# First attention: GpSimd in place of VectorE multiplies the probabilities by the inverse of their sum

## Chip, core and metric

One core of a Trainium2 chip (trn2) runs the whole program in one launch. The metric is the device time of one execution in microseconds (us). The kernel before takes 2439.32 us, the median of 3 runs (2437.27 to 2439.40).

## What is computed

A first network of two layers (grouped attention with a sink and a context, then a retention layer, each with a gated feed-forward part and adaptive modulations), followed by a second network of two layers. The change concerns the attention of the first layer of the first network, for 256 tokens, 16 heads of 64 and 4 key heads. The softmax has one more term, the sink, in its sum. The image tokens look at 512 keys, the context tokens at 256.

```python
s_ctx = jnp.einsum('bqkgd,bnkd->bkgqn', qb, k_c, preferred_element_type=jnp.float32) * scale
s_loc = jnp.einsum('bqkgd,bnkd->bkgqn', qb, kb, preferred_element_type=jnp.float32) * scale
s_loc = jnp.where(valid, s_loc, NEG_INF)
sink_col = jnp.broadcast_to(sink_g, s_ctx.shape[:-1] + (1,))
p = jax.nn.softmax(jnp.concatenate([s_ctx, s_loc, sink_col], axis=-1), axis=-1).astype(vb.dtype)
return (jnp.einsum('bkgqn,bnkd->bqkgd', p[..., :L], v_c)
        + jnp.einsum('bkgqn,bnkd->bqkgd', p[..., L:L + band], vb))
...
s_c = jnp.einsum('bqkgd,bnkd->bkgqn', q_c, k_c, preferred_element_type=jnp.float32) * scale
p_c = jax.nn.softmax(jnp.concatenate([s_c, sink_col], axis=-1), axis=-1).astype(v_c.dtype)
o_c = jnp.einsum('bkgqn,bnkd->bqkgd', p_c[..., :L], v_c)
```

## The kernel before

The program is written by hand, one instruction stream for each engine, and the streams meet at semaphores. SyncE streams the weights into four slots; ScalarE and VectorE split each into a high and a low part (lines 1653 and 2275); TensorE multiplies (lines 1060 to 1071). The attention stands between the query projection `q0` and the output projection `wo0`.

`heads_first` (line 617) lists the work of the first attention as blocks: for each of 8 pairs of heads one block for the image tokens (512 keys) and one for the context tokens (256 keys). A block has two steps, one for each half of 128 queries, and a step has two items, one for each head of the pair. So there are 32 steps and 64 items; of four steps in a row two are 512 keys wide and two 256. All four engines run the same function `attention`, each its own part, over the steps s; an engine works on several steps at once, by the lags `N_LAG` = 1, `T_LAG` = 2, `O_LAG` = 4 (line 677):

- **TensorE** (line 1252): scores of step s into three banks of PSUM used in turn; in every odd step side products of the modulation weights (line 1154, until these run out); the transposes of the probabilities of step s - 2 (line 1270, `wk` for the first item and `acc` for the second), which wait for `pn_ok` of their item; in every even step the product with the values (line 1288).
- **VectorE**: copies the sinks beside the probabilities' tile (line 2431), scales and masks the scores and takes their maximum in one instruction for each item (line 2440, into `probs`), makes the negative maximum (line 2444, two inputs in SBUF); then, for step s - 1, the reciprocal of the sums (line 2453, `rec_ok`) and, for each item, the multiply of the probabilities by it, in place (line 2459, `pn_ok`). The order of the instructions on the engine is that of the code.
- **ScalarE**: copies the transposed probabilities of step s - 2 out of PSUM (line 1859, `pt_ok`), then takes the exponentials of step s and their sum (line 1841, `p_ok`).
- **GpSimd** has nothing in this stretch. Behind it in its queue stand the sums of squares of `wo0` (`both_squares`, line 925), which wait for ScalarE's squares of that projection, and DMAs that follow these.

`probs` has 6 tiles, three steps of items. VectorE may write step s into them when the transposes of step s - 3 are done (`t_ok`, line 2431 waits). The inverse sums `srec` are a ring of 8. In the second network the same function runs again, with `again` true; there GpSimd makes the bias tiles (line 978) beside it, and VectorE's multiply stays as it is.

Of the kernel before, what the change touches and what calls it, by code (L numbers as in the profile page):

```python
# [23 lines left out]
ALU = mybir.AluOpType  # L24
# [328 lines left out]
PROBS, PROBS_T, SINK = 6, 4, 4  # L353
# [22 lines left out]
def pooled_both(name, n):  # L376

    return 5 * BOTH.index(name) + 2 * n + 1


def squared_before(name, l):

    first = [5 if n in BOTH else 4 for n in SQUARED1]
    if name in SQUARED1:
        return sum(first[:SQUARED1.index(name)])
    return sum(first) + 4 * SQUARED2.index(name) + l * 4 * len(SQUARED2)


def build(nc, a, out, const_at):
    J = JOBS  # L390
    st = ExitStack()
    with st:
        def sb(name, shape, dt=F32, on=st):
            return on.enter_context(nc.sbuf_tensor(name, shape, dt))

        def sem(name):
            return st.enter_context(nc.semaphore(name))
# [42 lines left out]
        smx, snm, ssum, srec = [sb(f"soft_{k}", [P, 8]) for k in ("mx", "nm", "sum", "rec")]  # L440
# [6 lines left out]
        def arena(*parts):  # L447
            with ExitStack() as on:
                return [sb(n, s, d, on) for n, s, d in parts]
# [4 lines left out]
        nf, nf_c, rows_c, prm_rows, ada_in, _, ada_s, c_pad, extra = arena(  # L454
            ("nf", [P, DC, S], F32), ("nf_c", [P, DC, S], F32), ("rows_c", [P, 2 * D], F32), ("prm_rows", [P, 4, P], F32),
            ("ada_in", [P, 2 * SLOTS, KCH, COLS], F32), ("ada_skip", [P, 592], F32), ("ada_s", [P, 4, COLS], F32),
            ("c_pad", [P, DC, 62], F32), ("extra", [P, EXTRA, KCH, COLS], F32))
# [5 lines left out]
        probs_t, probs = arena(("p_skip", [P, 10 * 2 * S + 4 * 256 + 4 * 2 * S], F32), ("probs_t", [P, PROBS_T, 4, S], F32),  # L463
                               ("probs", [P, PROBS, 2 * S + SINK], F32))[1:]
# [76 lines left out]
        s_ok, m_raw, m_ok, p_ok, rec_ok, pn_ok, t_ok, pt_ok, neg_ok = [sem(k) for k in (  # L541
            "s_ok", "m_raw", "m_ok", "p_ok", "rec_ok", "pn_ok", "t_ok", "pt_ok", "neg_ok")]
# [74 lines left out]
        def heads_first():  # L617

            bs = []
            for p in range(HEADS // 2):  # L620
                for ctx in range(2):
                    keys = slice(S, 2 * S) if ctx else slice(0, 2 * S)
                    tiles = range(2, 4) if ctx else range(4)
                    o = o_ps[p % 2]
                    gs = []
                    for n in range(2):
                        h, half = 2 * p + n, slice(64 * n, 64 * n + 64)
                        gs.append(dict(
                            q=[qk[half, p, ctx * S + r * P:ctx * S + (r + 1) * P] for r in range(2)],
                            k=[k_dup[half, h // GROUP, keys]] * 2, nk=[keys.stop - keys.start] * 2, rows=[slice(0, S)] * len(tiles), mask=[window[:, r, keys] for r in range(2)],  # L630
                            sink=(sinks, sinks_neg, 2 * p), scale=[q_inv[:, 2 * ctx + r, h:h + 1] for r in range(2)], probs=probs, probs_t=probs_t, pair=p,
                            v=[v_tok[:, t, 64 * (h // GROUP):64 * (h // GROUP) + 64] for t in tiles],
                            out=o[half, ctx * S:(ctx + 1) * S]))
                    bs.append((gs, [(p, o[:, 0:2 * S], h_hi[:, p, :], h_lo[:, p, :])] if ctx else []))
            return bs
# [34 lines left out]
        def attn_base(which, l):  # L670

            if which == "first":
                return 0, 0, 0
            return ITEMS0 + l * (ITEMS_WIN + ITEMS_MEM), PAIRS0 + l * (PAIRS_WIN + PAIRS_MEM), BLOCKS0 + l * BLOCKS2
# [4 lines left out]
        def attn_steps(blocks):  # L679
            return range(2 * len(blocks) + L_LAG - 1)  # L680
# [196 lines left out]
        def _(pool):  # L877
# [34 lines left out]
            pool.dma_start(window[:].rearrange("p r k -> p (r k)"), const("window")).then_inc(in_attn, 16)  # L912

            pool.wait_ge(x_done, X_START)
            def both_squares(name):

                k = pooled_both(name, 0)
                for n in range(3):
                    pool.wait_ge(sqb_ok, squared_before(name, None) + n + 1)
                    for c in range(2):  # L920
                        if n == 0 and c == 0:
                            continue
                        if n:
                            pool.wait_ge(both_ok, k + 2 * n - 2 + c)
                        pool.tensor_tensor(sq_total, act_buf[:, c, :], sq_total if n else act_buf[:, 0, :], ALU.add).then_inc(both_ok, 1)
# [34 lines left out]
            for l in range(LAYERS2):  # L960
# [4 lines left out]
                first, _, _ = attn_base("second", l)  # L965
# [1304 lines left out]
        def _(dve):  # L2270
# [146 lines left out]
            def attention(which, blocks, l=None, beside=None, ready=None):  # L2417
                first, pair0, _ = attn_base(which, l)
                again = which != "first"
                steps = 2 * len(blocks)  # L2420
                for s in attn_steps(blocks):
                    if s < steps:
                        gs, _ = blocks[s // 2]
                        i, c, sink = 2 * s, 2 * s % 8, gs[0]["sink"]
                        if i >= PROBS or again:
                            dve.wait_ge(t_ok, first + i - PROBS + 2)
                        if not s:
                            dve.wait_ge(*ready)
                        if sink is not None:
                            nk = gs[0]["nk"][s % 2]  # L2430
                            dve.tensor_copy(gs[0]["probs"][:, i % PROBS:i % PROBS + 2, nk:nk + 1], sink[0][:, sink[2]:sink[2] + 2].unsqueeze(2))
                        for n, G in enumerate(gs):
                            k = c + n
                            dve.wait_ge(s_ok, first + i + n + 1)
                            if again and G["bias"] is not None:
                                dve.wait_ge(bias_ok, 1 + G["bias"] + l * WH)
                            if again:
                                dve.memset(passed[:, k:k + 1], 0.0)

                            dve.tensor_tensor_reduce(G["probs"][:, (i + n) % PROBS, 0:G["nk"][s % 2]], (sc_ps[n] if again else sc_first[(i + n) % 3])[:, 0:G["nk"][s % 2]], G["mask"][s % 2], G["scale"][s % 2],  # L2440
                                                     -3.0e38, ALU.add, ALU.max, smx[:, k:k + 1]).then_inc(m_raw, 1)
                        dve.wait_ge(m_raw, first + i + 2)
                        if sink is not None:
                            dve.scalar_tensor_tensor(snm[:, c:c + 2], smx[:, c:c + 2], -1.0, sink[1][:, sink[2]:sink[2] + 2], ALU.mult, ALU.min)\  # L2444
                                .then_inc(m_ok, 2)
                        else:
                            dve.tensor_scalar(snm[:, c:c + 2], smx[:, c:c + 2], -1.0, None, ALU.mult).then_inc(m_ok, 2)
                    t = s - N_LAG
                    if 0 <= t < steps:
                        gs, _ = blocks[t // 2]  # L2450
                        j, k = 2 * t, 2 * t % 8
                        dve.wait_ge(p_ok, first + j + 2)
                        dve.reciprocal(srec[:, k:k + 2], ssum[:, k:k + 2]).then_inc(rec_ok, 2)
                        for n, G in enumerate(gs):
                            j = 2 * t + n
                            k = j % 8
                            dve.wait_ge(rec_ok, first + j + 1)
                            pr = G["probs"][:, j % PROBS, 0:G["nk"][t % 2]]
                            dve.tensor_scalar(pr, pr, srec[:, k:k + 1], None, ALU.mult).then_inc(pn_ok, 1)
                    q = block_at(s, L_LAG, blocks)  # L2460
                    if q is not None:
                        for pair, o, hi, lo in blocks[q][1]:
                            dve.wait_ge(o_hi_ok, pair0 + pair + 1)
                            dve.tensor_tensor(lo, o, hi, ALU.subtract).then_inc(o_done, 1)
                    if beside:
                        beside(2 * s)
                        beside(2 * s + 1)
# [228 lines left out]
            for j in range(STAGES):  # L2696
                dve.wait_ge(ada_sum, j + 1)
                stage_modulations(j)
                for kc in range(2 * j, 2 * j + 2):
# [5 lines left out]
                    for half in range(2):  # L2705
                        dve.wait_ge(nh_ok, 2 * kc + half + 1)
                        t = slice(half * S, half * S + S)
# [52 lines left out]
            n = [1]  # L2760
# [391 lines left out]
```

## Time and profile before

| | |
|---|---|
| median of 3 runs | 2439.32 us (2437.27 to 2439.40) |
| the profiled execution, its span | 2440.7 us, 1.4 above the median |
| TensorE busy | 2382.8 us (98%) |
| VectorE busy | 1560.6 us (64%) |
| ScalarE busy | 1213.9 us (50%) |
| GpSimd busy | 158.3 us (6%) |
| first attention | from 118 to 225 us of the span |

The profile is one execution with every instruction's start and duration. Busy is the time in which an engine has an instruction under way. The matmuls of TensorE overlap one another and their ends are modelled, so for TensorE the start of the next instruction tells more than a duration. "Idle before, released by" names the instruction whose semaphore came last. The chain is followed back from the last instruction of a stretch. Lines are those of the kernel before; in the changed kernel the lines of VectorE stand 13 further down. PE is TensorE, PEld its weight loads, DVE VectorE, ACT ScalarE, POOL GpSimd and SP SyncE.

### The profile page before, as it was taken

How to read it: one execution, taken by the hardware profiler on the slowest of the kernel's cores; microseconds unless marked ns; L12 is line 12 of the kernel's file. 1: busy time of each engine (PE TensorE's matmuls, PEld its weight loads, DVE VectorE, ACT ScalarE, POOL GpSimd, SP SyncE). 2: the span in 40 equal slices, each digit the busy share in tenths (PEclk: the TensorE clock that was granted, in tenths of full speed). 3: DMA queues.
4: the chain of work that ended last, by engine and by line, in shares of the span. 5: the costliest groups of instructions: out<-in, count | busy, mean ns of one | idle time of the engine just before them, and what ended most of it. 6: DMA issues, size and time to landing. Idle time of an engine off the chain costs nothing.

```text
span 2440.7 us, 39475 instructions
## 1 busy us (share of the span) xinstructions
PE 2382.8 (98%) x14178; PEld 2039.3 (84%) x14178; DVE 1560.6 (64%) x2316; ACT 1213.9 (50%) x1784; POOL 158.3 (6%) x145
## 2 busy tenths in 40 slices
PE   7999999999999999999999999999999999999999
PEld 6745788888788868888888899998888889989887
DVE  5377556432453366766876858777677766677774
ACT  4366422222343434555554586555455556865553
POOL 3000100000000000000000012100000000221000
PEclk9999999999999999999999999999999999999999
DMA  9453755433242424655656655456566565535654
GB/s 315 139 187 109 231 154 163 147 106 95 88 129 93 140 70 148 199 165 187 203 170 194 190 166 172 130 173 190 178 190 189 177 196 166 180 127 153 200 169 150
DMA packets 388418, 398.36 MB, mean 163 GB/s; under 512 B 17344, under 2 KB 382432, under 8 KB 388304
## 3 DMA queue, kind: packets, MB, share of 16 engines
q1 hardware_dynamic: 381984, 377.67, 50.4%
q0 software_dynamic: 6320, 19.17, 2.6%
q8 instruction: 72, 1.18, 0.2%
q14 instruction: 42, 0.34, 0.0%
HBM read 395.73 MB, written 1.05 MB: 163 GB/s over the span
## 4 chain that ended last, share of the span: by engine, by line
PE 87%; DVE 5%; issue 3%; ACT 2%; POOL 2%; DMA 0%; SPq 0%; ACTq 0%; DVEq 0%; POOLq 0%
PE acc L1060 29%; PE acc L1071 24%; PE acc L1064 18%; PE wk L1135 2%; PE acc L1135 2%; DVE w_lo L2275 1%; PE wk L1252 1%; ACT w_hi L1653 1%; PE acc L1605 1%; PE acc L1288 1%; PE wk L1288 1%; PE wk L1270 1%; PE wk L1154 1%; POOL bias L978 1%; PE wk L1496 1%
## 5 line engine op out<-in xcount | busy, mean ns | idle before, releaser
L2275 DVE TENSOR_TENSOR w_lo<-raw,w_hi 128x1024 fp32r<-128x1024 f32 (+1 forms) x656 | 816.0, 1258 | 503.8 <-ACT w_hi L1653 502.3
L1653 ACT CAST w_hi<-raw 128x1024 fp32r<-128x1024 f32 (+1 forms) x650 | 663.2, 1033 | 477.0 <-PE acc L1071 362.8
L1060 PE MATMUL acc<-h_all,w_hi 128*128 128x512 f32 x2328 | 586.0, 393 | 3.1 <-DVE h_all L2403 2.3
L1071 PE MATMUL acc<-h_all,w_lo 128*128 128x256 f32 (+1 forms) x3688 | 572.7, 298 | 0.0
L1071 PEld LDWEIGHTS acc<-h_all,w_lo 128*128 128x128 f32 x3688 | 525.2, 191 | 43.4
L1060 PEld LDWEIGHTS acc<-h_all,w_hi 128*128 128x128 f32 x2328 | 419.1, 189 | 80.4 <-issue 2.5
L1064 PE MATMUL acc<-h_all,w_hi 128*128 128x256 f32 (+1 forms) x2720 | 472.0, 326 | 10.6 <-DVE rot L2614 4.8
L1064 PEld LDWEIGHTS acc<-h_all,w_hi 128*128 128x128 f32 x2720 | 407.1, 192 | 55.6 <-issue 14.6
L1060 PE MATMUL acc<-hid_all,w_hi 128*128 128x512 f32 x880 | 221.5, 392 | 0.0
L1060 PEld LDWEIGHTS acc<-hid_all,w_hi 128*128 128x128 f32 x880 | 156.8, 188 | 26.8
L1071 PEld LDWEIGHTS acc<-hid_all,w_lo 128*128 128x128 f32 x1056 | 152.6, 188 | 17.0
L1071 PE MATMUL acc<-hid_all,w_lo 128*128 128x256 f32 (+1 forms) x1056 | 166.2, 297 | 0.0
L2572 DVE TENSOR_TENSOR act_buf<-acc,act_buf 128x512 f32<-128x512 f32 x110 | 76.0, 691 | 83.4 <-ACT act_buf L1935 54.0
L1064 PE MATMUL acc<-hid_all,w_hi 128*128 128x512 f32 x352 | 84.6, 392 | 0.0
L1935 ACT COPY act_buf<-acc 128x512 f32<-128x512 f32 x55 | 32.3, 587 | 95.3 <-PE acc L1071 95.3
L1064 PEld LDWEIGHTS acc<-hid_all,w_hi 128*128 128x128 f32 x352 | 66.0, 188 | 14.3
L1841 ACT ACTIVATE probs<-probs,soft_nm 128x257 f32<-128x257 f32 (+3 forms) x112 | 61.5, 554 | 21.2 <-DVE soft_nm L2444 18.1
L946 POOL TENSOR_TENSOR act_buf<-act_buf 128x512 f32<-128x512 f32 x8 | 10.4, 1299 | 860.6 <-ACT act_buf L1899 860.6
L2575 DVE TENSOR_TENSOR act_buf<-act_buf,rstd 128x512 f32<-128x512 f32 x88 | 60.9, 692 | 3.0
L1933 ACT COPY act_buf<-acc 128x512 f32<-128x512 f32 x55 | 32.2, 585 | 59.6 <-PE acc L1071 59.6
L1135 PE MATMUL wk<-w_hi,h_all 128*128 128x512 f32 x192 | 60.7, 393 | 0.1
L1945 ACT CAST hid_all<-act_buf 128x512 f32 (+1 forms) x55 | 34.2, 622 | 47.1 <-DVE act_buf L2580 46.3
(429 smaller groups left out, 2281.3 us busy)
## 6 DMA issues: line engine op xcount, KB each, us to landing
raw<-in_w_in_dram SPq DMA_DIRECT2D x100, 512.0 KB, 4.0
raw<-in_ffn_w_in_dram SPq DMA_DIRECT2D x88, 512.0 KB, 4.2
raw<-in_ffn_w_gate_dram SPq DMA_DIRECT2D x88, 512.0 KB, 4.4
raw<-in_ffn_w_up_dram SPq DMA_DIRECT2D x88, 512.0 KB, 4.3
raw<-in_ffn_w_down_dram SPq DMA_DIRECT2D x80, 512.0 KB, 4.1
raw<-in_ret_w_qkvg_dram SPq DMA_DIRECT2D x48, 512.0 KB, 3.7
raw<-in_ffn_w_out_dram SPq DMA_DIRECT2D x40, 512.0 KB, 3.5
ring<-in_ada_w_dram SPq DMA_DIRECT2D x34, 512.0 KB, 4.8
```

Source lines behind the costliest of these rows:

```text
L1060: pe.matmul(outs[cb], w_hi[:, s, k, c], merged[:, :, kk, t], start=(u == 0 and k == 0), stop=False, skip_group_check=True)
L1064: pe.matmul(outs[cb], w_hi[:, s, k, c], x[:, kk, t], start=(u == 0 and k == 0 and x is hi), stop=False, skip_group_check=True)
L1071: mm = pe.matmul(o, w_lo[:, s, k, cb * P:(cb + 1) * P], x[:, u * KCH + k, t], start=False, stop=(last and k == nk - 1), skip_group_check=True)
L1135: mm = pe.matmul(banks[n], xs[:, kk, x], ws[:, 2 * u:2 * u + 2, k, :], start=(kk == 0 and i == 0), stop=(kk == DC - 1 and i == 2))
L1288: mm = pe.matmul(G["out"][:, seen], G["v"][c], G["probs_t"][:, 2 * (q % 2) + n, c, seen], start=(c == 0), stop=(c == tiles - 1), skip_grou ...
L1653: act.copy(w_hi[:, s, 0:nk, :], raw[:, s, 0:nk, :]).then_inc(hi_done, 1)
L1841: act.activation(pr, pr, ACT.Exp, bias=snm[:, i % 8:i % 8 + 1], accum_out=ssum[:, i % 8:i % 8 + 1])\
L1935: act.copy(up, acc[:, 1, :, S:2 * S]).then_inc(low_ok, 1)
L1945: act.copy(hid_hi[:, bass.ts(it, 2), 0:S], buf).then_inc(hid_hi_ok, 1)
L2275: dve.tensor_tensor(w_lo[:, s, 0:nk, :], raw[:, s, 0:nk, :], w_hi[:, s, 0:nk, :], ALU.subtract).then_inc(lo_done, 1)
L2572: dve.tensor_tensor(part, acc[:, b, :, 0:S], part, ALU.add).then_inc(acc_free, 1)
L2575: dve.tensor_tensor(part, part, scale, ALU.mult).then_inc(gu_ok if b else gz_ok, 1)
```

## The change

GpSimd gets, after its last DMAs of the preparation, a loop over all 64 items of the first attention. For each it waits until the reciprocal is there (`rec_ok`), multiplies the item's probabilities in place, and reports it (`pn_ok`). VectorE skips its multiplies when the attention is the first, and with them its own wait for the reciprocal. TensorE waits for the same semaphore as before, at the same values.

```diff
             pool.wait_ge(x_done, X_START)
+
+            def normalise_first(blocks):
+
+                for t in range(2 * len(blocks)):
+                    gs, _ = blocks[t // 2]
+                    for n, G in enumerate(gs):
+                        j = 2 * t + n
+                        pool.wait_ge(rec_ok, j + 1)
+                        pr = G["probs"][:, j % PROBS, 0:G["nk"][t % 2]]
+                        pool.tensor_scalar(pr, pr, srec[:, j % 8:j % 8 + 1], None, ALU.mult).then_inc(pn_ok, 1)
+
+            normalise_first(heads_first())
+
             def both_squares(name):
...
                         dve.wait_ge(p_ok, first + j + 2)
                         dve.reciprocal(srec[:, k:k + 2], ssum[:, k:k + 2]).then_inc(rec_ok, 2)
-                        for n, G in enumerate(gs):
+                        for n, G in enumerate(gs if again else []):
                             j = 2 * t + n
                             k = j % 8
                             dve.wait_ge(rec_ok, first + j + 1)
```

On VectorE, before, where a step of 512 keys is followed by steps of 256 (`soft_nm` is the negative maximum, `soft_rec` the inverse sum; ISA is the instruction of line 2440, its second row the read of the maximum):

```order
L2444 SCALAR_TENSOR_TENSOR soft_nm<-soft_mx,sinks_neg 128x2
L2453 RECIPROCAL soft_rec<-soft_sum 128x2
L2459 TENSOR_SCALAR probs<-probs,soft_rec 128x512 x2
L2431 COPY probs<-sinks 128x2
L2440 ISA probs,soft_mx<-acc,act_buf,q_inv 128x256
L2440 ISA soft_mx 128x1
L2440 ISA probs,soft_mx<-wk,act_buf,q_inv 128x256
```

And the same place now:

```order
L2457 SCALAR_TENSOR_TENSOR soft_nm<-soft_mx,sinks_neg 128x2
L2466 RECIPROCAL soft_rec<-soft_sum 128x2
L2444 COPY probs<-sinks 128x2
L2453 ISA probs,soft_mx<-acc,act_buf,q_inv 128x256
L2453 ISA soft_mx 128x1
```

The two multiplies between the reciprocal and the next step's copy are gone; the rest keeps its order. On GpSimd, before, at the end of its preparation:

```order
L911 DMA sin_a<-in_shape_constants_dram 128x256
L912 DMA act_buf<-in_shape_constants_dram 128x1024
L925 ISA
L925 TENSOR_TENSOR rows<-act_buf 128x512 [waits sqb_ok,x_done]
L925 TENSOR_TENSOR rows<-act_buf,rows 128x512 [waits both_ok,sqb_ok]
```

And now (the squares follow after all 64 multiplies):

```order
L924 ISA
L924 TENSOR_SCALAR probs<-probs,soft_rec 128x512 [waits rec_ok,x_done]
L924 TENSOR_SCALAR probs<-probs,soft_rec 128x512 [waits rec_ok] x3
L924 TENSOR_SCALAR probs<-probs,soft_rec 128x256 [waits rec_ok] x4
L924 TENSOR_SCALAR probs<-probs,soft_rec 128x512 [waits rec_ok] x4
```

The multiplies stand in the queue ahead of the squares, each with a wait of its own.

## Rows read from the trace of the kernel before

**Rows 1.** The page, span and busy time of each engine with its share

```profile
span 2440.7 us, 39475 instructions
...
PE 2382.8 (98%) x14178; PEld 2039.3 (84%) x14178; DVE 1560.6 (64%) x2316; ACT 1213.9 (50%) x1784; POOL 158.3 (6%) x145
```

**Rows 2.** Chain of waits through the first attention, 118 to 225 us

```profile
by line: PE wk L1252 13.7%; PE wk L1270 12.3%; PE acc L1288 10.9%; PE wk L1288 10.8%; DVE probs L2440 10.8%; PE acc L1154 9.0%; PE acc L1252 8.3%; PE acc L1270 7.8%; DVE probs L2459 4.1%; issue 3.4%; PE wk L1154 1.9%; DVE soft_rec L2453 1.3
```

**Rows 3.** Windows: length, busy us of PE, PEld, DVE, ACT, POOL, clock, DMA

```profile
150.00:161.76 11.76, 11.56 (x100) 6.13 (x98) 9.63 (x38) 8.61 (x26) 0.00 (x0) 1.00 0.75 244
```

**Rows 4.** Timeline of TensorE, one pair: start us, us, instruction

```profile
147.99 0.44 PE L1270 MATMUL wk<-ident,probs 128*128 128x128 f32 x2
...
150.45 1.13 PE L1252 MATMUL wk<-k_dup,qk 64*128 64x512 f32 x4
...
152.51 0.44 PE L1270 MATMUL wk<-ident,probs 128*128 128x128 f32 x2
...
153.99 0.66 PE L1270 MATMUL wk<-ident,probs 128*128 128x128 f32 x4 [0.20 <-DVE probs L2459]
154.49 0.60 PE L1270 MATMUL acc<-ident,probs 128*128 128x128 f32 x4
...
157.66 0.66 PE L1270 MATMUL wk<-ident,probs 128*128 128x128 f32 x4
158.16 0.60 PE L1270 MATMUL acc<-ident,probs 128*128 128x128 f32 x4
```

**Rows 5.** Timeline of VectorE, the same stretch

```profile
146.31 0.62 DVE L2459 TENSOR_SCALAR probs<-probs,soft_rec 128x256 f32<-128x256 f32 x2
...
149.93 0.62 DVE L2459 TENSOR_SCALAR probs<-probs,soft_rec 128x256 f32<-128x256 f32 x2
...
151.61 0.75 DVE L2440 CUSTOM_DVE_ANT_0 probs<-wk,act_buf,q_inv 128x512 f32<-128x512 f32 x1 [0.39 <-PE wk L1252]
...
153.25 0.17 DVE L2453 RECIPROCAL soft_rec<-soft_sum 128x2 f32<-128x2 f32 x1
153.45 0.88 DVE L2459 TENSOR_SCALAR probs<-probs,soft_rec 128x512 f32<-128x512 f32 x2
...
155.62 0.88 DVE L2459 TENSOR_SCALAR probs<-probs,soft_rec 128x512 f32<-128x512 f32 x2
```

**Rows 6.** Waits in the first attention: total us, times, longest us

```profile
PE wk L1270 <- DVE probs L2459: 3.4, 8, 0.9
...
PE wk L1252 <- DVE soft_mx L2440: 1.6, 1, 1.6
```

**Rows 7.** Groups by line and shape: count, busy us, mean ns, idle before

```profile
L2459 DVE TENSOR_SCALAR probs<-probs,soft_rec 128x512 f32<-128x512 f32 x32 | 14.1, 484 | 0.7 <-DVE soft_rec L2453 0.2
...
L946 POOL TENSOR_TENSOR act_buf<-act_buf 128x512 f32<-128x512 f32 x8 | 10.4, 1299 | 860.6 <-ACT act_buf L1899 860.6
...
L964 POOL TENSOR_TENSOR GI<-GI,XC 128x2048 f32<-128x2048 f32 x2 | 9.2, 4623 | 230.4 <-ACT gates L1990 230.4
```

**Rows 8.** Timelines of GpSimd and VectorE in the second network's attention

```profile
1513.90 2.04 POOL L978 TENSOR_TENSOR bias<-alibi,slopes 128x512 f32<-128x512 f32 x2 [5.59 <-DVE soft_mx L2440]
...
1511.42 0.16 DVE L2444 SCALAR_TENSOR_TENSOR soft_nm<-soft_mx,sink_neg_l 128x2 f32<-128x2 f32 x1
...
1513.73 0.08 DVE L2440 DVE_READ_ACCUMULATOR2_ANT soft_mx<- 128x1 f32 x1
1513.93 1.02 DVE L2444 SCALAR_TENSOR_TENSOR soft_nm<-soft_mx,sink_neg_l 128x2 f32<-128x2 f32 x1
...
1515.06 1.15 DVE L2459 TENSOR_SCALAR probs<-probs,soft_rec 128x128 f32<-128x128 f32 x2
...
1526.50 0.48 DVE L2459 TENSOR_SCALAR probs<-probs,soft_rec 128x128 f32<-128x128 f32 x2
```

**Rows 9.** Timelines of GpSimd and TensorE at the last branch product

```profile
1581.98 1.56 POOL L983 TENSOR_TENSOR h_all<-gates,h_all 128x512 fp32r<-128x512 f32 x1 [1.30 <-ACT h_all L2019]
...
1583.67 1.57 PE L1064 MATMUL acc<-h_all,w_hi 128*128 128x256 f32 x11 [1.00 <-POOL h_all L983]
```

## Prediction

> **What bounds the kernel now.** I read the page first, then the stretch of the first attention (118 to 225 us), then one period of it instruction by instruction. The span is 2440.7 us, and GpSimd works 158.3 us of it, 6% [rows 1]. The change touches nothing outside the first attention, so its effect is a few us or parts of one per step, summed over the 32 steps.
>
> The chain through that stretch is mostly TensorE: score, transpose and value matmuls (lines 1252, 1270, 1288) and the side products (1154). VectorE is on it with the maxima (2440, 10.8%) and with the multiply that is moved (2459, 4.1%) [rows 2]. One pair of heads is four steps and repeats every 11.76 us; in the window of one such period TensorE is busy 11.56, VectorE 9.63, ScalarE 8.61 and GpSimd 0.00 us [rows 3]. So TensorE is the bound, and VectorE is not, although it is busy 82%.
>
> The reader should see how TensorE meets the multiply. In each step it writes scores, runs side work, and only then transposes the probabilities of two steps back. Take the pair whose second scores start at 150.45. The group of transposes at 153.99 is the one place of the four where TensorE is late on VectorE: its row says 0.20 idle, released by line 2459 [rows 4]. On VectorE the maxima start at 151.61 (after 0.39 of idle, so VectorE itself waited for scores), the reciprocal at 153.25 and the two multiplies at 153.45, 0.88 together [rows 5]. The first ends at 153.45 + 0.48 = 153.93, TensorE starts 0.06 later. In all, TensorE waits for line 2459 only 3.4 us here, and 1.6 us once for a maximum near the start [rows 6].
>
> **What is removed.** VectorE loses 64 multiplies: 16 steps of 0.88 and 16 of 0.62, that is 24.0 us of its busy time [rows 5, 7]. I cost that at nothing. Maxima cannot start before their scores, VectorE already idles before them, and the scores are in TensorE's order behind transposes and side work. If this cover is wrong, the most to gain is the waits on VectorE just named, 3.4 + 1.6 = 5.0 us, 0.2%. The additions below eat them first.
>
> **What is added.** GpSimd gets the same 64 multiplies, each waiting for the reciprocal. Nothing else stands in its queue meanwhile: the next thing there is the squares of the output projection, after attention. No DMA is moved past it, the SP queue is unchanged. The price is the latency from reciprocal to transpose. It is the sum of three things:
> - VectorE to GpSimd: a maximum read out at 1513.73 for 0.08 released GpSimd at 1513.90, so 0.09 us [rows 8].
> - D, the duration of one 128x512 multiply on GpSimd. No row shows a tensor_scalar there.
> - GpSimd to TensorE: the add at 1581.98 takes 1.56 and the matmul starts at 1583.67, so 0.13 us, where VectorE had 0.06 [rows 9].
>
> **D bounded.** From above by the two-input product or sum of the same shape, 1.30 [rows 7]. From below by VectorE's own 0.48; nothing excludes that GpSimd is as quick. Between them are two better guides. The bias (line 978) is also a tile times one value per partition, issued with that value as a second, repeated input: two take 2.04, so 1.02 each [rows 8]. And two-input ops of 512 and 2048 columns take 1.30 and 4.62 [rows 7]: 2.16 ns a column over 0.19 fixed. If one input costs half of that per column, D is 0.19 + 512 x 1.08 = 0.74, an estimate. I take the middle of 0.74 and 1.02, D = 0.88.
>
> The Trainium skill, "GPSIMD Engine Reference", section 4.1, puts one-input work on GpSimd roughly at line rate, and section 3.1 gives 1.03 cycles an element at 1.2 GHz for short bodies. By that figure D would be an estimated 0.44 plus the fixed part, 0.63, and the sum would be about 3 us instead of 7. No row here shows it, since every GpSimd row has two inputs.
>
> **The sum.** In the pair above the reciprocal ends at 153.25 + 0.17 = 153.42. GpSimd starts at 153.51 (0.06 after VectorE did), ends the second multiply at 153.51 + 2D, and TensorE can transpose that item at 153.64 + 2D. Before, it did so at 154.49 [rows 4]. The delay per pair is 2D - 0.85. (The first item gives D - 0.35, which is smaller once D is over 0.50.) With D = 0.88 this is 0.91 us per pair.
>
> The other three groups have slack. The second 128x512 group (multiplies at 155.62, transposes at 157.66 and, for its second item, 158.16) would be ready at about 155.68 + 1.76 + 0.13 = 157.57. The first 128x256 group (146.31, transposes 147.99, second item 0.27 later) with 0.54 each is ready at 146.37 + 1.08 + 0.13 = 147.58. The last (149.93, transposes 152.51) has over a microsecond more [rows 4, 5]. So one group in four pays.
>
> Seven pairs pay: 7 x 0.91 = 6.4 us. The first pair is different: TensorE waits there for a later maximum, behind six small rope products of VectorE that now need not wait for two multiplies (0.88 less) but partly stand behind GpSimd (below); I put it at 0, from -0.5 to +0.7. The last pairs have no side products to cover a group: there one more may pay the difference of the multiplies, 0.88 - 0.48 = 0.40, so +0.4, an estimate. The sum is +6.8 us. TensorE is the bound from there to the end, so all of it arrives. Against the span it gives 2447.5; the runs' median is 1.4 below the span, so 2439.3 + 6.8, rounded to **2446.0 us**.
>
> **GpSimd and VectorE hold each other up.** When the bias started at 1513.90, VectorE's 128x2 line 2444, which takes 0.16 otherwise, took 1.02, and the two 128x128 multiplies behind it 1.15 in place of 0.48 [rows 8]. With the change such a stall can fall on line 2444 of the next step: its two maxima take at least 0.96 us, GpSimd is busy 1.76 after the reciprocal, so VectorE stands some 0.3 to 0.8 us. This delays only exponentials and multiplies with 0.6 us of slack or more, and VectorE has just given up 0.62 to 0.88 in each step. I cost it at 0 with D = 0.88.
>
> **Rivals.**
> 1. *GpSimd is quick, D from 0.48 to 0.68.* For: one input instead of two. Against: no row below 1.02. The sum is 7 x (2D - 0.85) + 0.4, so +1.2 to +4.0 us: 2440.5 to 2443.3, no change. Chance 0.32. This is where the page's rate lands.
> 2. *Slow, and the lock bites.* D = 1.30, as with two inputs. Per pair 1.75; then the slack of the second 128x512 group is gone too (155.68 + 2.60 + 0.13 = 158.41 against 158.16) and the stalls of line 2444 join: 7 x 1.75 + 1 to 3 = 13 to 15 us, 2453 to 2454. For: the lock is in the trace. Against: the bias takes 1.02. Chance 0.10. The Trainium skill, "SBUF — State Buffer", section "Who interferes with whom", states that the second to issue blocks fully; by that the trace agrees (1.02 for 0.16), and it adds copies to the ops that can be held, which no run here shows.
> 3. *Faster.* The mechanism is VectorE's relief at the start and in the steps without side products: line 2459 no longer stands before the maxima that TensorE waits for (1.6 us once), and per pair 0.2 us of wait is won. It decides if D is under 0.43, where 2D - 0.85 turns negative and the two multiplies beat VectorE's 0.88. Then up to 5.0 us come back: about 2435. Against: VectorE's own instruction takes 0.48. Chance 0.05.
> 4. *The change does not move the work:* the order of instructions shows 32 pairs gone from VectorE and 64 on GpSimd, so no chance is kept for this.
>
> **How the numbers follow.** Forecast case, D from 0.68 to 1.15, +4 to +11 us, mostly slower by over 0.2% (4.9 us, about what a measurement of this kernel can tell from no change): chance 0.53. Its low end, D under 0.74, stays within 4.9 us and gives 0.05 to "same". Slower: 0.48 + 0.10 = 0.58. Same: 0.32 + 0.05 = 0.37. Faster: 0.05. The range runs from the lower bound of D, 2440.5, to 2452.5, just short of the two-input price; it leaves out rivals 2 and 3 and little else.
>
> **What would show it.** In the changed profile: 64 multiplies on GpSimd, none of line 2459's on VectorE in the stretch; their start-to-start time in a step is D. The wait of line 1270's transposes for GpSimd should be near 0.2 + 0.9 once a pair at the first 128x512 group, the period 12.7 instead of 11.76 us, VectorE's busy time 24 us lower, and line 2444 should have single instances near D. The prediction is wrong if the period stays 11.8 (D small), if transposes wait in more than one group of four, or if a later stretch takes the delay back.

## The result, and the profile after

The changed kernel takes **2463.32 us** (median of 4 runs, 2462.65 to 2466.57) against 2439.36 for the kernel before on the same chip (4 runs). The ratio is 1.0098, with a 95% interval of 1.0085 to 1.0111: slower by 24 us. The forecast was 2446.0 with a range up to 2452.5, so the direction came true and the size did not; the loss is 3.6 times what was forecast (24.0 against 6.7).

The head of the changed kernel's page, which answers to [rows 1]:

```profile
span 2461.3 us, 39475 instructions
...
PE 2389.8 (97%) x14178; PEld 2042.2 (83%) x14178; DVE 1539.1 (63%) x2252; ACT 1215.3 (49%) x1784; POOL 237.0 (10%) x209
```

The span is 20.6 us longer. The 64 instructions have moved (DVE x2316 to x2252, POOL x145 to x209). VectorE gave up 21.5 us, and GpSimd took on 78.7.

The groups by line and shape of the changed kernel in its first attention (118 to 250 us); columns: count, busy us, mean ns of one, idle before and its releaser:

```profile
L924 POOL TENSOR_SCALAR probs<-probs,soft_rec 128x512 f32<-128x512 f32 x32 | 49.6, 1566 | 88.5 <-DVE soft_rec L2466 88.5
L924 POOL TENSOR_SCALAR probs<-probs,soft_rec 128x256 f32<-128x256 f32 x32 | 29.2, 926 | 21.6 <-DVE soft_rec L2466 21.6
```

This is the term that the forecast did not have a row for: D is **1.57 us**, not 0.88, and above even the two-input instruction that was taken as the upper bound, 1.30 [rows 7]. In 256 columns it takes 0.93 where VectorE took 0.31 (two in 0.62, [rows 5]).

TensorE's waits in that stretch (total us, times, longest), to be held against [rows 6]; the transposes are now line 1283, the maxima 2453, the reciprocal 2466:

```profile
PE wk L1283 <- POOL probs L924: 13.3, 9, 2.0
PE acc L1283 <- POOL probs L924: 7.9, 11, 0.9
```

Together 21.2 us of waiting for GpSimd, where TensorE had waited 3.4 + 1.6 = 5.0 us for VectorE. The windows of two periods, columns as in [rows 3]:

```profile
167.10:181.15 14.05, 11.83 (x98) 6.10 (x97) 7.01 (x31) 8.88 (x27) 9.89 (x9) 1.00 0.31 103
181.15:195.20 14.05, 11.84 (x98) 6.11 (x97) 6.96 (x30) 8.83 (x27) 9.84 (x9) 1.00 0.00 1
```

A pair takes 14.05 us instead of 11.76, at the same granted clock, 1.00. TensorE is busy 11.84 of it, and no engine is busy throughout: the period is now set by a chain, not by an engine. One such period in detail, TensorE first (start, us, instruction, idle before and its releaser), to be held against [rows 4]:

```profile
185.83 0.66 PE L1283 MATMUL wk<-ident,probs 128*128 128x128 f32 x4 [1.33 <-POOL probs L924]
187.37 0.66 PE L1283 MATMUL acc<-ident,probs 128*128 128x128 f32 x4 [0.88 <-POOL probs L924]
...
190.61 0.66 PE L1283 MATMUL wk<-ident,probs 128*128 128x128 f32 x4
```

and VectorE and GpSimd in the same period:

```profile
183.95 0.17 DVE L2466 RECIPROCAL soft_rec<-soft_sum 128x2 f32<-128x2 f32 x1
...
185.53 0.16 DVE L2457 SCALAR_TENSOR_TENSOR soft_nm<-soft_mx,sinks_neg 128x2 f32<-128x2 f32 x1
```

```profile
184.21 6.19 POOL L924 TENSOR_SCALAR probs<-probs,soft_rec 128x512 f32<-128x512 f32 x4 [1.74 <-DVE soft_rec L2466]
```

The reader should see the chain: reciprocal ends at 184.12, GpSimd starts at 184.21 (0.09, as forecast), its first multiply is done after 6.19/4 = 1.55 at 185.76, and TensorE starts at 185.83. The second multiply ends at 187.31 and TensorE's second group starts at 187.37. The next row of 512 keys (190.61) does not wait: GpSimd has finished it at 190.40. So the forecast's picture, one exposed group in four, is what the trace shows: of the 20 waits on GpSimd above, 16 are the two items of the eight exposed groups. The other four, 1.7 us together, are the second item of a 256 group at 149.27 (0.20), of a 512 group at 218.56 (0.19), and a 256 group near the end (0.83 and 0.47, shown further down).

### The profile page after: what moved, and what is told of

Read it like the earlier page. It is cut to its first block, busy times and chain, and to the rows that moved or that the text cites. A ratio compares the mean times of both kernels' runs of the same rounds, so it can differ in the third digit from the quotient of the medians.

```text
span 2461.3 us, 39475 instructions
## 1 busy us (share of the span) xinstructions
PE 2389.8 (97%) x14178; PEld 2042.2 (83%) x14178; DVE 1539.1 (63%) x2252; ACT 1215.3 (49%) x1784; POOL 237.0 (10%) x209
## 3 DMA queue, kind: packets, MB, share of 16 engines
HBM read 395.73 MB, written 1.05 MB: 161 GB/s over the span
## 4 chain that ended last, share of the span: by engine, by line
PE 85%; DVE 5%; issue 3%; POOL 3%; ACT 2%; SPq 1%; DMA 1%; ACTq 0%; DVEq 0%; POOLq 0%
PE acc L1073 30%; PE acc L1084 24%; PE acc L1077 17%; PE wk L1148 2%; PE acc L1148 2%; POOL probs L924 1%; SPq L780 1%; DVE w_lo L2288 1%; PE wk L1265 1%; PE acc L1618 1%; ACT w_hi L1666 1%; PE wk L1301 1%; PE acc L1301 1%; DVE probs L2453 1%; POOL bias L991 1%
## 5 line engine op out<-in xcount | busy, mean ns | idle before, releaser
L924 POOL TENSOR_SCALAR probs<-probs,soft_rec 128x512 f32<-128x512 f32 (+1 forms) x64 | 78.8, 1246 | 110.1 <-DVE soft_rec L2466 110.1
```

What stands on the lines that cost most here:

```text
L924: pool.tensor_scalar(pr, pr, srec[:, j % 8:j % 8 + 1], None, ALU.mult).then_inc(pn_ok, 1)
```

## The experiments

The theory: the loss is the latency from the reciprocal to the first group of 512 keys in each pair, 2D - 0.85 a pair with D = 1.55 (the pitch of two multiplies). The rivals: the sum of 64 slow multiplies wherever they stand, including a second group of 512 whose slack is gone; contention between GpSimd and VectorE that makes D what it is; and the change of VectorE's order.

**1. Another form of the same multiply.** All 64 stay on GpSimd, as a product of two tensors, the second being the column repeated:

```diff
-                        pool.tensor_scalar(pr, pr, srec[:, j % 8:j % 8 + 1], None, ALU.mult).then_inc(pn_ok, 1)
+                        pool.tensor_tensor(pr, pr, srec[:, j % 8:j % 8 + 1].broadcast_to((P, G["nk"][t % 2])), ALU.mult).then_inc(pn_ok, 1)
```

> All 64 multiplies stay on GpSimd, but as a tensor_tensor whose second input is the inverse sum repeated along the row, the form of the bias op that took 1.02 us. Duration theory (the loss is the time of one GpSimd multiply in the latency from reciprocal to transpose, 2D - 0.85 a pair): D 1.02 to 1.3 instead of 1.57, so period 12.9 to 13.5 us instead of 14.05 and +10 to +15 us over before, not +24. Lock theory (the loss is VectorE and GpSimd holding each other up at the shared port, per instruction): as many instructions hold it, with two streams instead of one, so +20 us or more. Clock theory (waits of TensorE bring its clock down and that makes a good part of the loss): waits still come in every pair, so low stretches remain and the time stays over +15.

Measured: 2452.01 us against 2439.94, ratio 1.0047 [1.0031, 1.0064]. Half of the loss is gone (12.1 us left). Its groups and waits in the same stretch:

```profile
L924 POOL TENSOR_TENSOR probs<-probs,soft_rec 128x512 f32<-128x512 f32 x32 | 32.7, 1046 | 96.4 <-DVE soft_rec L2466 96.4
L924 POOL TENSOR_TENSOR probs<-probs,soft_rec 128x256 f32<-128x256 f32 x32 | 18.9, 612 | 31.2 <-DVE soft_rec L2466 31.2
```

```profile
PE wk L1283 <- POOL probs L924: 9.1, 9, 1.5
PE acc L1283 <- POOL probs L924: 2.9, 8, 0.5
```

With two inputs the same product takes 1.05 us, as the bias did [rows 8]. The period is 12.92 (from 163.67 to 176.59), 1.16 more than before; 2 x 1.02 - 0.85 gives 1.19, with 1.02 the pitch of two. The formula holds at a second value of D. The 12.1 us lie in the range of the duration theory, and below what the lock theory (+20 or more) and the clock theory (over +15) of the expectation asked for. This run also shows what the forecast expected of the lock. VectorE's timeline while two multiplies of GpSimd are under way (166.72 to 168.76):

```profile
166.72 2.04 POOL L924 TENSOR_TENSOR probs<-probs,soft_rec 128x512 f32<-128x512 f32 x2 [2.34 <-DVE soft_rec L2466]
```

```profile
168.05 0.72 DVE L2457 SCALAR_TENSOR_TENSOR soft_nm<-soft_mx,sinks_neg 128x2 f32<-128x2 f32 x1
```

That instruction, 0.16 otherwise, ends when the second multiply does. In the changed kernel itself its like at 185.53 took 0.16 in the middle of GpSimd's work (above).

**2 and 3. Only one of the two lengths on GpSimd.** VectorE keeps the others, in its old place; a second semaphore tells the two apart. The function's return value chooses the steps, and only this line differs between runs 2, 3, 5 and 6:

```diff
+        def pooled_item(t, n):
+            return t // 2 % 2 == 0
...
+                        if not pooled_item(t, n):
+                            continue
...
-                            pe.wait_ge(pn_ok, first + j + 1)
+                            pe.wait_ge(*normalised(again, first, j))
...
-                        for n, G in enumerate(gs if again else []):
+                        for n, G in enumerate(gs):
+                            if not again and pooled_item(t, n):
+                                continue
```

(`== 0`: the steps of 512 keys, run 2; `== 1`: those of 256, run 3.)

> GpSimd multiplies only in the steps of 512 keys (32 of 64 items), VectorE does the others. Duration theory: all of the loss but 2 to 3 us, since the one exposed group of a pair is a 512 one: +18 to +21 us, period 14.0. Lock theory: the load on the port is 49.6 of 78.8 us, so about 60% of the loss, +13 to +15.

> GpSimd multiplies only in the steps of 256 keys (the other 32 items). Duration theory: their transposes have over a microsecond of slack, so +0 to +3 us, period 11.8. Lock theory: 29.2 of 78.8 us of port time, so +8 to +9 us.

Measured: run 2, 2462.95, ratio 1.0100 [1.0083, 1.0117], the whole loss (23.0 us, where +18 to +21 was expected). Run 3, 2442.32 (10 runs) against 2439.94, 1.0008 [0.9999, 1.0018]: 2.4 us more, not told from no change. TensorE's waits of run 3, with VectorE's old wait back:

```profile
PE wk L1297 <- DVE probs L2488: 3.3, 8, 0.9
PE wk L1297 <- POOL probs L938: 2.0, 2, 1.7
```

So 32 multiplies of 256 columns on GpSimd, each three times as long as VectorE's, cost at most a few us. The waits for GpSimd that are left stand in the last two pairs: 0.29 at 203.27, and 1.70 and 0.46 at a 256 group near the end (215.43). So the time of 32 slow multiplies as such is not the price.

**4. The disputed cost by itself.** The kernel before, with 27 multiplies put on GpSimd between 50 and 82 us in a buffer that is free then, after a fill of it: three lengths, three forms, each waiting for the one before. They are additional work and change nothing that is computed.

```diff
+            for n in (512, 256, 128):
+                for k in range(3):
+                    probed(pool.tensor_scalar(probe[:, 0:n], probe[:, 0:n], col, None, ALU.mult))
+                for k in range(3):
+                    probed(pool.tensor_scalar(stage[:, 0:n], stage[:, 0:n], 1.0, None, ALU.mult))
+                for k in range(3):
+                    probed(pool.tensor_tensor(probe[:, 0:n], probe[:, 0:n], col.broadcast_to((P, n)), ALU.mult))
```

> The kernel before, plus 27 probe instructions on GpSimd while it is idle (50 to 118 us), three each of 512, 256 and 128 columns in three forms: tensor_scalar with the scalar from SBUF, tensor_scalar with an immediate, tensor_tensor with a repeated column. The time should stay within 2 us of before. If the form is the price: the first 1.5 / 0.9 us at 512 / 256 columns also with nobody beside it, the third about 1.02 at 512. If instead contention made the multiplies of the change long, the first takes clearly less than 1.5 here. The immediate form tells whether the scalar read from SBUF is what costs.

Measured (one execution, 2438.55 us). Line 930 multiplies by a column, 932 by a constant, 934 by the repeated column. First a multiply by a column while VectorE does nothing (in the window 56 to 57 us VectorE is busy 0.00):

```profile
L930 POOL TENSOR_SCALAR rows<-rows,ones 128x512 f32<-128x512 f32 x1 | 1.6, 1563 | 0.1
```

Then by a constant, 57.3 to 59 us; VectorE is not idle here (busy 1.37 of 1.70):

```profile
L932 POOL TENSOR_SCALAR rows<-rows 128x512 f32<-128x512 f32 x2 | 3.0, 1496 | 0.2
```

By the repeated column, 61 to 65.6 us (VectorE 0.00):

```profile
L934 POOL TENSOR_TENSOR rows<-rows,ones 128x512 f32<-128x512 f32 x3 | 3.1, 1040 | 0.2
```

And 128 columns, 76 to 79 us (VectorE busy 0.81 of 3.00):

```profile
L930 POOL TENSOR_SCALAR rows<-rows,ones 128x128 f32<-128x128 f32 x3 | 1.8, 604 | 0.3
L932 POOL TENSOR_SCALAR rows<-rows 128x128 f32<-128x128 f32 x2 | 1.1, 528 | 0.2
```

So the tensor-by-scalar form is slow by itself: 1.56 us with nobody beside it, the 1.57 of the changed kernel. It is slow with a constant too (1.50), and the two-input form of the same product is faster (1.04). The scalar's place in memory and the attention around it have little part in D. Beside VectorE's two-input work some probes were much slower, though. The first three by a column, at 50.64, took 6.65 us together, 1.81, 3.09 and 1.56 one by one; the last of them is the one above.

```profile
50.64 6.65 POOL L930 TENSOR_SCALAR rows<-rows,ones 128x512 f32<-128x512 f32 x3
```

VectorE was busy 4.96 us of that window, and its two products of 128x1024 that start at 53.13 took 2.70 us where they take 2.29 in the kernel before: both engines lose. The form is not what decides this: of the two-input probes of 256 columns, 0.61 each, one took 1.69 while VectorE worked on such a product (73.55). In the attention before the change VectorE has one such product, and D there hardly varies (run 2: 1.55 to 1.62 in all 32).

**5 and 6. A quarter of the multiplies, and the other three quarters.** `return t % 4 == 0` moves only the first step of 512 keys of each pair (16 multiplies), `t % 4 != 0` the other 48.

> GpSimd multiplies only in the first 512-key step of each pair (16 of 64 items, t % 4 == 0), with tensor_scalar. Exposed-group theory: this is the group whose transposes TensorE reaches with no slack, so nearly the whole loss with a quarter of the instructions: +18 to +21 us, period 14.0. If instead each multiply on GpSimd costs its share, +6.

> GpSimd multiplies in the other three steps of each pair (48 items). Exposed-group theory with D 1.55: the second 512 group would be ready at 155.68 + 3.10 + 0.13 = 158.91 against 158.16, so it now pays 0.75 us a pair, and in the last pairs without side products more: +8 to +11 us, period 12.5 to 12.8. Share theory: +18.

Measured: run 5, 2462.13 against 2440.34, ratio 1.0088 [1.0071, 1.0105], slightly over the +18 to +21 expected. Run 6, 2449.15 (10 runs), 1.0032 [1.0022, 1.0041]. Sixteen instructions carry 21.8 us of the loss, the other forty-eight 8.8 on their own. TensorE's waits in run 5:

```profile
PE wk L1297 <- POOL probs L938: 12.4, 8, 2.0
PE acc L1297 <- POOL probs L938: 8.2, 8, 1.2
```

Each of the eight pairs waits twice, 2.6 us in all. VectorE keeps its other 48 multiplies here, in their old places, so taking those away from it is not what costs; run 8 below takes all 64 away and loses nothing. Run 6's 8.8 us answers the question of the second group of 512. In its timeline of TensorE the first group is VectorE's again, and the second item of the second group is late:

```profile
164.78 0.66 PE L1297 MATMUL wk<-ident,probs 128*128 128x128 f32 x4 [0.19 <-DVE probs L2488]
...
169.62 0.66 PE L1297 MATMUL acc<-ident,probs 128*128 128x128 f32 x4 [0.52 <-POOL probs L938]
```

The two do not add up (21.8 + 8.8 = 30.6 against 24.0): where the first group is late, everything on TensorE behind it is late too, and the second group finds its slack again. In run 6 the pair takes 12.50 us (152.28 to 164.78 between first groups), 0.74 more than before; the forecast's arithmetic gave 0.75.

**7. Earlier reciprocals.** If latency from the reciprocal is the loss, then moving the reciprocal should win it back. In the changed kernel VectorE takes the reciprocal of the exposed step ahead of the next step's two maxima instead of behind them:

```diff
+                    if not again and 0 <= s - N_LAG < steps and rec_early(s - N_LAG):
+                        inverse_sums(s - N_LAG)
                     if s < steps:
...
-                        dve.wait_ge(p_ok, first + j + 2)
-                        dve.reciprocal(srec[:, k:k + 2], ssum[:, k:k + 2]).then_inc(rec_ok, 2)
+                        if again or not rec_early(t):
+                            inverse_sums(t)
```

(`rec_early(t)` is `t % 4 == 0`; `inverse_sums` is the two lines taken out.)

> The changed kernel, but VectorE takes the reciprocal of the first 512 step (t % 4 == 0) ahead of the next step's maxima instead of behind them, so GpSimd can start about 1.5 us earlier in the exposed group. Exposed-group theory: the latency there shrinks, the second 512 group becomes the exposed one: period 12.6 instead of 14.05, +12 to +15 us over before. If the GpSimd time as such is the cost, +24 as in the changed kernel.

Measured: 2446.5 us (10 runs), 1.0024 [1.0015, 1.0034], period 12.3. The loss is 6.2 us where +12 to +15 was expected, so three quarters of it come back (17.8 of 24.0). The rows show what is left of it, and that in this pair it is still the first group's second item, not the second group, that waits. GpSimd and TensorE in one pair:

```profile
161.61 4.91 POOL L924 TENSOR_SCALAR probs<-probs,soft_rec 128x256 f32<-128x256 f32 x4 [1.90 <-DVE soft_rec L2440]
```

```profile
165.36 0.66 PE L1283 MATMUL wk<-ident,probs 128*128 128x128 f32 x4
166.57 0.66 PE L1283 MATMUL acc<-ident,probs 128*128 128x128 f32 x4 [0.56 <-POOL probs L924]
```

The reciprocal is there at 163.07 + 0.17 = 163.24, but GpSimd works without a gap from 161.61 to 166.52: the two multiplies of 256 (2 x 0.92) occupy it until about 163.45, and the two of 512 follow. The latency is hidden now up to GpSimd's own queue, with 0.56 left.

**8. Both: earlier reciprocals and the two-input form.**

> As the one before, with the multiply as tensor_tensor with the repeated inverse (1.05 / 0.61 us). Exposed-group theory: no 512 group is exposed any more, period 11.7 as before or below; +2 to +4 us from the first and last pairs. Then GpSimd's 51 us of multiplies are hidden nearly whole. Otherwise +12 as with the broadcast form alone.

Measured: 2438.53 us (10 runs), ratio 0.9990 [0.9980, 1.0000], where +2 to +4 us was expected. All 64 multiplies are on GpSimd, and nothing of the loss is left. The window of one period:

```profile
150.00:161.50 11.50, 11.50 (x100) 6.14 (x98) 7.55 (x29) 8.73 (x26) 6.44 (x8) 1.00 1.06 344
```

TensorE is busy all 11.50 us of it: the period is TensorE's work again, 0.26 shorter than before the change. The same kernel was run once more, in five rounds, beside runs 9 and 10:

> The reciprocal-first broadcast kernel once more with more rounds: all on GpSimd. Period 11.50; 1 to 3 us faster than before (0.9990 to 0.9996), an interval that may or may not leave out 1.

Measured: 2438.27 against 2440.12, ratio 0.9991 [0.9982, 1.0000], as the first time: no worse than before the change, and less than 0.2% better.

**9 and 10. What is GpSimd's part in that?** Run 9 is the kernel before with the reciprocal moved alone. Run 10 has the reciprocal moved, and only the first step of 512 keys on GpSimd in the two-input form; VectorE does the rest.

> Control: the kernel before, VectorE multiplies everything, only the reciprocal of the first 512 step of a pair stands ahead of the next step's maxima. The multiplies stay behind the maxima, so only the 0.1 to 0.2 us of the reciprocal leave the exposed latency: period 11.6 to 11.7 instead of 11.76, 0 to 1 us faster, not to be told from no change. If this alone gives what the reciprocal-first broadcast kernel gave (about 2 us), GpSimd has no part in that gain.

> The best use of GpSimd by the exposed-group theory: it multiplies only the first 512 step of each pair, in the broadcast form and with the reciprocal ahead of the maxima; VectorE keeps the others. Period 11.5 to 11.6, all pairs without a wait there, 1 to 3 us faster than before. If the reciprocal-first order is not what matters, it pays as the first-512 kernel did, +10 or more with D 1.05.

Measured: run 9, 2437.87 against 2440.12, ratio 0.9993 [0.9984, 1.0002], not told from no change, period 11.53, shorter than the 11.6 to 11.7 expected. Run 10, 2435.33, **0.9979 [0.9970, 0.9988]**, period 11.50. Run 10's timeline of GpSimd and the two groups of transposes behind it:

```profile
160.64 2.04 POOL L938 TENSOR_TENSOR probs<-probs,soft_rec 128x512 f32<-128x512 f32 x2 [9.46 <-DVE soft_rec L2454]
```

```profile
162.69 0.66 PE L1297 MATMUL wk<-ident,probs 128*128 128x128 f32 x4
163.18 0.60 PE L1297 MATMUL acc<-ident,probs 128*128 128x128 f32 x4
```

Run 10 is faster than both kernels, by 4.8 us than before and by 28 than the changed one. The order of the reciprocal gives nearly all of the shorter period (11.53 of run 9), and run 9 alone is as fast as the kernel of run 8 run beside it (2437.87 against 2438.27): by the expectation's own test GpSimd has no part that shows in the gain of run 8. Between run 9 and run 10 lie 2.5 us. Their intervals against before overlap, but 8 of the 11 executions of run 10 are below the fastest of run 9 (2436.58), so the difference between them is probably real. In the traces TensorE waits for VectorE's multiply four times in run 9 (1.9 us) and once in run 10 (0.9 us). But the granted clock was also higher in run 10's trace (0.89 against 0.79 from 126 to 142 us), so what GpSimd adds to the new order is not settled here.

## Why the prediction was wrong, step by step

**What bounds the kernel: right.** TensorE was the bound, VectorE had room: its 21.5 us (24.0 forecast) bought nothing, and GpSimd being early or late is all that shows.

**The place and the formula: right.** "So one group in four pays" and 2D - 0.85 per pair: with the measured pitch of 1.55 the formula gives 2.25, and the period grew by 2.29. It held at 1.02 too (1.19 against 1.16), and the removal of the exposed step from GpSimd (run 6), of the others (run 5) and of the reciprocal's delay (runs 7 and 8) each moved the time in its direction. The two hand-offs, 0.09 and 0.13, measured 0.09 and 0.07 in the pair above: the first as taken, the second 0.06 shorter.

**D: wrong, and with it the number.** The step that failed is "D bounded. From above by the two-input product or sum of the same shape, 1.30", together with "if one input costs half of that per column". Neither was a bound: on this engine the tensor-by-scalar multiply costs (1566 - 926)/256 = 2.50 ns a column, against 2.16 for two tiles. The bias row, 1.02, was the right price of the wrong instruction, since it was issued with the value as a second, repeated input; run 1 gives that form 1.05. The argument that fewer inputs cannot cost more was the whole of the upper bound, and no row had it. What failed is thus a term of the sum that was mis-sized: D is 1.57 where 0.88 was put. With the pitch of 1.55 in it, the sum's main term is 7 x 2.25 = 15.8 instead of 6.4.

**The Trainium skill, "GPSIMD Engine Reference", sections 4.1 and 3.1**, puts one-input work roughly at line rate, and rival 1 had 0.63 from its figure. The measurement decides otherwise: 1.57 in the kernel, and 1.56 by a column and 1.50 by a constant in run 4.

**The slack of the other groups: right at D = 0.88, gone at 1.55, and covered.** The forecast's own sum puts the second group of 512 at 155.68 + 3.10 + 0.13 = 158.91 against 158.16, 0.75 late. Run 6 shows it when it stands alone: a wait of 0.52 before its second item, and a period longer by 0.74. In the changed kernel the first group's delay covers it (190.61 without a wait). The first 256 group is at its edge too: with 0.93 each the forecast's sum gives 146.37 + 1.86 + 0.13 = 148.36 against 148.26, and the changed kernel has one wait of 0.20 there (149.27).

**First pair and last pairs.** The first pair was put at 0. From the attention's first maximum to the first exposed group it was 7.99 us (118.48 to 126.47) and is 7.60 (118.05 to 125.65), so -0.4, within the range given. TensorE waits longer there for GpSimd (2.02, where it waited 0.78 for VectorE), but the granted clock before the change was lower in this stretch (0.80 from 118 to 126.5, against 1.00 to 126). The last pairs were put at +0.4, which was too small. From the last exposed group to the first matmul of the output projection it was 12.32 us (212.39 to 224.71) and is 15.75 (227.98 to 243.73): +3.4. Without side products the groups of 256 wait too, as in TensorE's timeline of the changed kernel:

```profile
227.98 0.66 PE L1283 MATMUL wk<-ident,probs 128*128 128x128 f32 x4 [2.01 <-POOL probs L924]
229.52 0.66 PE L1283 MATMUL acc<-ident,probs 128*128 128x128 f32 x4 [0.88 <-POOL probs L924]
...
235.26 0.44 PE L1283 MATMUL wk<-ident,probs 128*128 128x128 f32 x2 [0.83 <-POOL probs L924]
236.16 0.44 PE L1283 MATMUL acc<-ident,probs 128*128 128x128 f32 x2 [0.47 <-POOL probs L924]
```

**The sum again.** -0.4 + 15.8 + 3.4 = 18.8, against +19.45 for the attention, measured from its first maximum to the first matmul behind it (106.23 before, 125.68 after). The seven gaps between exposed groups really grew by 16.4, and with that the parts add up. The rest of the program took 1.2 us more, which makes the +20.6 of the span; that is within the spread of single executions. The agreement is better than the parts deserve, since the granted clock falls below 1.00 in some stretches of both executions (between 120 and 168 us 0.91 in the mean before, 0.89 after). One gap there took 15.77 us already before the change, against 11.76 in most others, and after it three took 14.56, 15.99 and 15.58 against 14.05: by these rows an estimate of 4.0 us lost in each execution, which cancels. At the end the clock was low only after the change (0.81 and 0.76 from 228 to 236 us, 1.00 before), and part of the 3.4 stands there. What the clock adds to the loss was not tried apart and stays open. The medians differ by 3.4 us more than the spans. An execution's time is about 1.8 us longer than its span (2463.05 and 2461.3 for the changed kernel's profiled one), so the profiled execution of before, span 2440.7, was an estimated 3.1 us above its median and not 1.4, while that of after was 0.3 below.

**The lock: wrong for this form.** It was expected on line 2444 with instances near D. In the changed kernel that instruction (now line 2457) is held once, by 0.22 us. All its instances in the first attention, then those of run 1; min/median/max in ns:

```profile
L2457 DVE SCALAR_TENSOR_TENSOR soft_nm<-soft_mx,sinks_neg x32: 160/161/382, 119.6 to 233.9; 128x2 f32<-128x2 f32 x32
```

```profile
L2457 DVE SCALAR_TENSOR_TENSOR soft_nm<-soft_mx,sinks_neg x32: 160/161/1003, 119.1 to 224.8; 128x2 f32<-128x2 f32 x32
...
L2444 DVE COPY probs<-sinks x32: 148/214/969, 117.4 to 220.9; 128x2 f32<-128x2 f32 x32
```

With the two-input form it is held up to 1.00 us, as in the second network [rows 8], and so is a copy of 128x2, up to 0.97. By that the trace agrees with the Trainium skill, "SBUF — State Buffer", section "Who interferes with whom", that the second to issue waits for the first, for the two-input form; that copies are among what is held is shown now too. With tensor-by-scalar the trace goes against it for the negative maximum, which has two inputs in SBUF and passed in 0.16 at 185.53 while GpSimd worked. That form does hold some short instructions, more briefly: copies of 128x2 take up to 0.42 us here and 0.52 in run 7, where none took over 0.17 before the change. In run 7 one at 163.15 ends at 163.46, together with GpSimd's multiply (161.61 + 2 x 0.92 = 163.45). Why the two forms differ stays open. The price of the lock was put at 0, and run 8, whose line 2467 (the negative maximum) is held up to 0.60 us, loses nothing.

**The rivals.** The nearest was the slow one, with D = 1.30 and 13 to 15 us. Its late second group came true where that group stands alone (run 6), its lock did not, and its D was still too small. It was given 0.10, which was too little for a price with no row.

## What to carry to other kernels

A range for a cost that no row shows has to come from the same instruction, not from a neighbour that looks harder; here fewer inputs were slower by a factor of 1.5, and one probe in an idle stretch would have told. A multiply moved to a slower engine costs the latency of its chain in the places where the consumer has no slack, and little elsewhere as long as the slack lasts: find those places (here 16 of 64 instructions), and look whether the producer's trigger can be issued earlier, before choosing the engine. Where the receiving engine works a queue in order, the trigger's lead is of use only up to the end of what stands before it in that queue.

## What the runs showed of the hardware that was not expected

- GpSimd's multiply of a 128-partition f32 tile by one value per partition takes 1.57, 0.93 and 0.60 us for 512, 256 and 128 columns, and by a constant 1.50 for 512 and 0.53 for 128. The same product with the value as a repeated second input takes 1.05 and 0.61 for 512 and 256, (1046 - 612)/256 = 1.70 ns a column. That is less also than the 1.30 of two full tiles of 512 columns [rows 7].
- A tensor-by-scalar on GpSimd holds VectorE's short instructions briefly or not at all (0.52 us at most in run 7 for 0.17). The two-input form holds them up to 1.00 us. Beside VectorE's products of 128x1024 GpSimd's own instructions stretch: one tensor-by-scalar of 1.57 took 3.09, one two-input of 0.61 took 1.69 (run 4).
- The period of 11.76 us before the change was not TensorE's floor. An instruction of 0.17 us, issued two maxima earlier, takes 0.23 us off each pair (run 9), though the whole time of that run is not told from before.
